# Attention's exponentials turned by a product with a diagonal of one over their sums

## The chip, the cores and the metric

The kernel runs on one core of one Trainium2 chip. The metric is device time of one execution in microseconds (us); the figure for a kernel is the median of its runs. Engines are named as in the profile: PE is TensorE's matmul row, PEld its weight loads, DVE is VectorE, ACT is ScalarE, POOL is GpSimd, SP is SyncE.

## What is computed

Two transformer-like blocks on 256 tokens of width 1024, all in 32-bit floats. The first block holds a forgetting attention with 8 heads of 128 (queries against keys, causal, two blocks of 128 queries), beside it a gated delta rule, and then a feed-forward part. The second holds an attention with 8 heads of 64 over a 4 x 64 grid, beside it a pooling, and again a feed-forward part. What matters here are the two softmaxes and the products that follow them:

```python
# forgetting attention, per head and block of 128 queries
s = jnp.einsum('bhqd,bhkd->bhqk', qi, kh).astype(jnp.float32) * scale
s = s + (ci[..., :, None] - c[..., None, :])
p = jax.nn.softmax(jnp.where(causal, s, -jnp.inf), axis=-1)
return jnp.einsum('bhqk,bhkd->bhqd', p.astype(vh.dtype), vh)
# neighbourhood attention, per head
p = jax.nn.softmax(s.reshape(B, H, GRID_W, wr * WIN_COLS), axis=-1)
return jnp.einsum('bqhwk,bwqkhd->bqhd', p, vg)
```

## The kernel before

The program is written out by hand for the five engines, one function for each: `tensor_program`, `scalar_program`, `vector_program`, `pool_program` and `sync_program`. All big products with weights go through one list of weight panels, cut into half panels (`HALVES`), and every engine walks the same steps n = 1, 2, ... `STEPS`, one for each half panel. In step n, PE does `gemm(n)`; ACT and DVE split the half panel of step n + 3 into a high part (`panel_hi`, line 946) and a rest (`panel_lo`, line 1385), and the high and low parts are multiplied in three products each. There are four buffers for half panels, so the splits stay up to three steps ahead of PE. Everything else is hung on fixed steps: after its big product, each engine does the small pieces that its tables name for this n. The order of every engine's queue is thus written out, and waits are on semaphores of the engine that makes or frees a buffer.

The forgetting attention ("fox") starts head hh at step 39 + 3 hh (`FOX_AT`). In that step PE makes the scores. One step later DVE adds the bias and takes the row maxima (`fox_bias`, line 1586, into `fox_p`, a ring of 3). Two steps later ACT takes exponentials in place and their row sums (`fox_exp`, line 1085). Three steps later DVE inverts the sums and multiplies them in (`fox_normalise`, lines 1590 to 1598). Four steps later PE turns the three 128 x 128 blocks of `fox_p` by transposes against the identity (`fox_turn`, line 769), and ACT copies the result from the PSUM bank to `fox_pT`. Five steps later PE multiplies with the values (`fox_values`); `fox_values(7)` comes in step 64, right behind the turning of head 7. The PSUM banks of scores, turned blocks and results of this attention are a ring of two. In the same steps DVE inverts small matrices for the delta rule (`blocks_X`, `blocks_T`, lines 1546 and 1549), and PE does that rule's products.

The neighbourhood attention ("na") is a staircase over v = 0 to 12 (`NA_AT`): scores and bias of head v, exponentials of head v - 1 (`na_exp`), normalising of head v - 2 (`na_normalise`, lines 1682 to 1689), turning of head v - 3 (`na_turn`, line 816, four blocks of 128 x 128), values from v - 5 on (`na_values`). In two steps more than one v is done with no big product between them (6 and 7, and 11 and 12). Its PSUM banks are a ring of four ("side"), its `na_p` a ring of four.

Of the kernel before, what the change touches and what calls it, by code (L numbers as in the profile page):

```python
# [19 lines left out]
ALU = mybir.AluOpType  # L20
# [3 lines left out]
P = 128  # L24
T = 256
TT = T // P
# [127 lines left out]
FOX_AT = {39 + 3 * hh: hh for hh in range(HEADS)}  # L154
# [30 lines left out]
def build(nc, a, out, scratch_a, scratch_x, scratch_c):  # L185
    ctx = ExitStack()
    with ctx:
        def sem(name):
            return ctx.enter_context(nc.semaphore(name))
# [3 lines left out]
        def at(name, shape, unit, dt=F32, skip=0):  # L193
            return nc.alloc_sbuf_tensor_at(name, shape, dt, offset=BASE + int(unit * UNIT) + skip)[:]
# [8 lines left out]
        fox_p = [at(f"fox_p{i}", [P, 3 * P], 10, skip=1536 * i) for i in range(3)]  # L203
# [53 lines left out]
        na_p = [at(f"na_p{i}", [P, TT, T], 13, skip=2048 * i) for i in range(4)]  # L257
        na_pT = [at(f"na_pT{i}", [P, TT, T], 14, skip=2048 * i) for i in range(4)]

        small_at = [BASE + 25 * UNIT]  # L260

        def small(name, shape, dt=F32, bytes_=4):
            n = bytes_
            for s in shape[1:]:
                n *= s
            t = nc.alloc_sbuf_tensor_at(name, shape, dt, offset=small_at[0])[:]
            small_at[0] += -(-n // 32) * 32
            return t
# [3 lines left out]
        cst = small("constants", [P, N_CONSTS])  # L272
        prm = small("params", [P, N_PARAMS])
        st = small("stats", [P, 176])

        blkA = at("blocks_A", [P, BLOCK, BLOCK], 0, skip=5120)
        blkX = at("blocks_X", [P, BLOCK, BLOCK], 0, skip=6144)
# [12 lines left out]
        def C(name):  # L290
            lo, hi = CONSTS[name]
            return cst[:, lo:hi]
# [5 lines left out]
        ident, upper, ones = C("ident"), C("upper"), C("ones")[:, 0:1].broadcast_to([P, P])  # L298
# [20 lines left out]
        nst = st[:, 48:48 + 32].rearrange("p (h c) -> p h c", c=4)  # L319
# [10 lines left out]
        def fox_stats(hh):  # L330
            return st[:, 128 + 4 * hh:130 + 4 * hh], st[:, 130 + 4 * hh:132 + 4 * hh]

        FOX_PARTS = [slice(0, P), slice(P, 3 * P)]
# [34 lines left out]
        def conv_rows(c):  # L368
# [36 lines left out]
        s_osq, s_oss, s_o_ms, s_o_rs = sem("o_squares"), sem("o_square_sums"), sem("o_means"), sem("o_rsqrt")  # L405
        s_ogz, s_on = sem("o_times_gz"), sem("o_normalised")
        s_yg_hi = sem("yg_hi")
        s_fox_exp, s_fox_rec, s_fox_norm = sem("fox_exp"), sem("fox_reciprocal"), sem("fox_normalised")
        s_yf_hi = sem("yf_hi")
        s_gate_f, s_gate_g, s_mixed, s_y_hi, s_y = (sem(n) for n in ("gate_f_affine", "gate_g_affine", "mixed", "y_hi",  # L410
                                                                      "y_lo"))
# [6 lines left out]
        s_h2_row, s_h2 = sem("h2_row_scaled"), sem("h2_gained")  # L418
        s_n_sq, s_n_ss, s_n_ms, s_n_rs, s_n_tok = (sem(f"qk2_{n}") for n in ("squares", "sums", "means", "rsqrt",
                                                                            "normalised"))  # L420
        s_na_exp, s_na_rec, s_na_norm = (sem(f"na_{n}") for n in ("exp", "reciprocal", "normalised"))
        s_na_hi, s_pool_hi = sem("na_hi"), sem("pooled_hi")
        s_g_tanh, s_g_stt, s_g_mul, s_g_hi, s_g_lo = (sem(f"ffn2_{n}") for n in ("tanh", "silu", "product", "hi", "lo"))
        s_out = sem("output_written")
# [7 lines left out]
        def bank_for(ring, key):  # L432
            while True:
                n = rings[ring][ring_at[ring] % len(rings[ring])]
                ring_at[ring] += 1
                if n not in held:
                    break
            place[key] = (n, uses[n])
            uses[n] += 1
            return banks[n]  # L440
# [4 lines left out]
        def room(key):  # L445
            n, use = place[key]
            return [(s_emptied[n], use)] if use else []

        def filled(key):
            return s_filled[place[key][0]], fill[key]  # L450
# [8 lines left out]
        def will_fill(key):  # L459
            n = place[key][0]  # L460
            times[n] += 1
            fill[key] = times[n]
            return s_filled[n]
# [8 lines left out]
        def side(key):  # L472
            return bank_for("side", key)
# [4 lines left out]
        def pairs(bank):  # L478
            return bank.rearrange("p (c t) -> p c t", c=2)
# [43 lines left out]
        def tensor_program(e):  # L523
# [238 lines left out]
            def fox_turn(hh):  # L762
                key = ("fox_t", hh)
                bank = bank_for("fox", key)
                for s, v in room(key):
                    e.wait_ge(s, v)
                e.wait_ge(s_fox_norm, hh + 1)
                for u in range(3):
                    i_ = e.transpose(bank[:, u * P:(u + 1) * P], fox_p[hh % 3][:, u * P:(u + 1) * P], ident)
                i_.then_inc(will_fill(key), 1)  # L770

            def fox_values(hh):
# [35 lines left out]
            def na_turn(hh):  # L808
                key = ("na_t", hh)
                c3 = pairs(side(key))  # L810
                for s, v in room(key):
                    e.wait_ge(s, v)
                e.wait_ge(s_na_norm, hh + 1)
                for k in range(2):
                    for m in range(TT):
                        i_ = e.transpose(c3[:, k, m * P:(m + 1) * P], na_p[hh % 4][:, m, k * P:(k + 1) * P], ident)  # L816
                i_.then_inc(will_fill(key), 1)

            def na_values(hh):
# [50 lines left out]
            for n in range(1, STEPS + 1):  # L870
# [37 lines left out]
                if n - 4 in FOX_AT:  # L908
                    fox_turn(FOX_AT[n - 4])
# [467 lines left out]
        def vector_program(e):  # L1377
# [209 lines left out]
                                                nm[:, m:m + 1])  # L1587
                i_.then_inc(empties(("fox_s", hh)), 1)

            def fox_normalise(hh):  # L1590
                _, sums = fox_stats(hh)
                pb = fox_p[hh % 3]
                e.wait_ge(s_fox_exp, hh + 1)
                e.reciprocal(sums, sums).then_inc(s_fox_rec, 1)
                e.wait_ge(s_fox_rec, hh + 1)
                for m, s in enumerate(FOX_PARTS):
                    i_ = e.tensor_scalar(pb[:, s], pb[:, s], sums[:, m:m + 1], None, ALU.mult)
                i_.then_inc(s_fox_norm, 1)

            def fox_lo(hh):  # L1600
                e.wait_ge(s_yf_hi, hh + 1)
# [68 lines left out]
            def na_bias(hh):  # L1670
                pb, nm = na_p[hh % 4], nst[:, hh, 0:2]
                b3 = pairs(bank_of(("na_s", hh)))
                if hh >= 4:
                    e.wait_ge(*filled(("na_t", hh - 4)))
                e.wait_ge(s_rpb_masked, hh + 1)
                e.wait_ge(*filled(("na_s", hh)))
                for m in range(TT):
                    i_ = e.tensor_tensor_reduce(pb[:, m, :], b3[:, m, :], bias2[:, hh, m, :], -1.0, -3 * NEG, ALU.add,
                                                ALU.min, nm[:, m:m + 1])
                i_.then_inc(empties(("na_s", hh)), 1)  # L1680

            def na_normalise(hh):
                pb, sums = na_p[hh % 4], nst[:, hh, 2:4]
                e.wait_ge(s_na_exp, hh + 1)
                e.reciprocal(sums, sums).then_inc(s_na_rec, 1)
                e.wait_ge(s_na_rec, hh + 1)
                for m in range(TT):
                    i_ = e.tensor_scalar(pb[:, m, :], pb[:, m, :], sums[:, m:m + 1], None, ALU.mult)
                i_.then_inc(s_na_norm, 1)

            def na_lo(hh):
                e.wait_ge(s_na_hi, hh // 2 + 1)
                e.tensor_tensor(mixl[:, hh // 2, :], bank_of(("na_y", hh // 2))[:, 0:T],
                                mixh[:, hh // 2, :].bitcast(F32), ALU.subtract).then_inc(empties(("na_y", hh // 2)), 1)

            def pool_mean(g):
                e.wait_ge(*filled(("pool_m", g)))
                e.tensor_copy(poolT[:, g, :], bank_of(("pool_m", g))[:, 0:T]).then_inc(empties(("pool_m", g)), 1)

            def pool_lo(g):  # L1700
                e.wait_ge(s_pool_hi, g + 1)
                e.scalar_tensor_tensor(mixl[:, 4 + g, :], bank_of(("pool_y", g))[:, 0:T], PR("pool_scale")[:, g:g + 1],
                                       mixh[:, 4 + g, :].bitcast(F32), ALU.mult, ALU.subtract) \
                    .then_inc(empties(("pool_y", g)), 1)
# [41 lines left out]
            for n in range(1, STEPS + 1):  # L1746
# [118 lines left out]
                if n - 5 in FOX_AT and FOX_AT[n - 5] < 7:  # L1865
                    fox_lo(FOX_AT[n - 5])
                if n - 3 in FOX_AT:
                    fox_normalise(FOX_AT[n - 3])
                if n - 1 in FOX_AT:
                    fox_bias(FOX_AT[n - 1])  # L1870
                for j in range(4):
# [74 lines left out]
                for v in NA_AT.get(n, ()):  # L1946
                    for hh in VALUES_AT.get(v, ()):
                        if hh % 2:
                            na_lo(hh)
                    if 0 <= v - 2 < HEADS:  # L1950
                        na_normalise(v - 2)
                    if 0 <= v < HEADS:
                        na_bias(v)
                    if v - 1 in POOL_AT:
                        pool_lo(POOL_AT[v - 1])
                    if v in POOL_AT:
                        pool_mean(POOL_AT[v])
# [203 lines left out]
        tensor_program(nc.tensor)  # L2161
        scalar_program(nc.scalar)
        vector_program(nc.vector)
        pool_program(nc.gpsimd)
        sync_program(nc.sync)
# [73 lines left out]
```

## Time and profile before

| | us |
|---|---|
| median of 3 runs | 850.86 (849.62 to 851.27) |
| the profiled execution | 851.71 |
| its span | 850.4 |
| PE busy in the span | 828.2 (97%) |
| DVE busy | 584.4 (69%) |
| ACT busy | 442.9 (52%) |
| POOL busy | 87.8 (10%) |

The profile is one execution. The span is what the profiler saw between the first and the last instruction; the profiled execution took 1.3 us more than it. Times in the views below are us from the start of the span. A row of a timeline gives the start, the time taken, engine, line, operation, output and inputs, the count of merged instructions, and in brackets how long the engine had sat idle before and what released it. A 32-bit product that is not a transpose stands in the trace as two matmuls with two weight loads, a transpose as one of each.

### The profile page before, as it was taken

What the parts mean: (1) busy time and instruction counts of PE and PEld (TensorE: products, weight loads), DVE (VectorE), ACT (ScalarE), POOL (GpSimd) and SP (SyncE); (2) the same over time, 40 slices, a digit from 0 to 9 for tenths busy, and PEclk for the clock granted to TensorE, in tenths of its full rate; (3) what the DMA queues carried; (4) which work ended last, traced back from release to release, by engine and by line L of the source; (5) the groups of instructions that cost most, each with busy time, mean ns of one, the idle gap of its engine ahead of it and who ended that gap; (6) DMA issues with size and microseconds to landing.
All of it is one profiled execution on the core that took longest, in us unless ns stands there. A gap on an engine that the chain in (4) does not pass through costs nothing.

```text
span 850.4 us, 14646 instructions
## 1 busy us (share of the span) xinstructions
PE 828.2 (97%) x5992; PEld 773.1 (91%) x5992; DVE 584.4 (69%) x930; ACT 442.9 (52%) x686; POOL 87.8 (10%) x70
## 2 busy tenths in 40 slices
PE   7899999999999999999999999998999999999998
PEld 5899999999998999899999988876767999999887
DVE  5788878784442756669999996586645766666543
ACT  5666577763344344456565563374554444444431
POOL 0001000101010401100211110133000101111000
PEclk9999999999999999999999999999999999999999
DMA  8754563646331465574777665645323755665542
GB/s 245 229 152 150 176 219 115 175 129 176 109 106 50 137 205 159 195 245 151 223 222 251 210 222 175 214 134 172 99 75 87 236 181 169 197 186 168 194 171 75
DMA packets 130707, 144.19 MB, mean 170 GB/s; under 512 B 11456, under 2 KB 111952, under 8 KB 130384
## 3 DMA queue, kind: packets, MB, share of 16 engines
q1 hardware_dynamic: 130640, 143.25, 53.4%
q8 instruction: 48, 0.79, 0.4%
q14 instruction: 19, 0.16, 0.1%
HBM read 141.78 MB, written 1.46 MB: 168 GB/s over the span
## 4 chain that ended last, share of the span: by engine, by line
PE 87%; DVE 5%; issue 3%; ACT 2%; POOL 1%; DMA 1%; SPq 0%; ACTq 0%; POOLq 0%; DVEq 0%
PE bank L525 84%; DVE panel_lo L1385 2%; DMA panel_raw<-in_w_in 1%; POOL stats L1973 1%; ACT panel_hi L946 1%; POOL o_tok L2023 1%; DVE xlo L1406 1%; DMA h<-in_x 1%; PE bank L816 1%; PE bank L566 0%; PE bank L588 0%; PE bank L641 0%; DVE blocks_T L1546 0%; DVE decayT L1448 0%; DVE h L1619 0%
## 5 line engine op out<-in xcount | busy, mean ns | idle before, releaser
L1385 DVE TENSOR_TENSOR panel_lo<-panel_raw,panel_hi 128x1024 fp32r<-128x1024 f32 x252 | 327.2, 1301 | 178.1 <-ACT panel_hi L946 177.2
L946 ACT ACTIVATE panel_hi<-panel_raw 128x1024 fp32r<-128x1024 f32 x252 | 266.7, 1060 | 220.6 <-PE bank L525 214.0
L525 PE MATMUL bank<-xhi,panel_hi 128*128 128x256 f32 x1152 | 329.5, 286 | 4.3 <-ACT conv_acc L946 2.4
L525 PE MATMUL bank<-xhi,panel_lo 128*128 128x256 f32 x1152 | 325.9, 283 | 0.0
L525 PE MATMUL bank<-xlo,panel_hi 128*128 128x256 f32 x1152 | 325.9, 283 | 0.0
L525 PEld LDWEIGHTS bank<-xhi,panel_hi 128*128 128x128 f32 x1152 | 220.9, 192 | 5.2 <-ACT conv_acc L946 2.6
L525 PEld LDWEIGHTS bank<-xlo,panel_hi 128*128 128x128 f32 x1152 | 221.0, 192 | 0.2
L525 PEld LDWEIGHTS bank<-xhi,panel_lo 128*128 128x128 f32 x1152 | 220.9, 192 | 0.0
L525 PE MATMUL bank<-panel_hi,act_hi 128*128 128x512 f32 x176 | 68.6, 390 | 0.0
L525 PE MATMUL bank<-panel_hi,act_lo 128*128 128x512 f32 x176 | 68.5, 389 | 0.0
L525 PE MATMUL bank<-panel_lo,act_hi 128*128 128x512 f32 x176 | 68.5, 389 | 0.0
L525 PE MATMUL bank<-panel_hi,xhi 128*128 128x256 f32 (+1 forms) x192 | 63.8, 333 | 0.8 <-DVE xlo L1406 0.8
L525 PE MATMUL bank<-panel_hi,xlo 128*128 128x256 f32 (+1 forms) x192 | 61.8, 322 | 0.0
L525 PE MATMUL bank<-panel_lo,xhi 128*128 128x256 f32 (+1 forms) x192 | 61.7, 321 | 0.0
L525 PEld LDWEIGHTS bank<-panel_hi,xhi 128*128 128x128 f32 x192 | 36.8, 192 | 4.7 <-issue 2.2
L525 PEld LDWEIGHTS bank<-panel_lo,xhi 128*128 128x128 f32 x192 | 36.9, 192 | 2.8
L525 PEld LDWEIGHTS bank<-panel_hi,act_hi 128*128 128x128 f32 x176 | 33.0, 188 | 6.8
L525 PEld LDWEIGHTS bank<-panel_lo,act_hi 128*128 128x128 f32 x176 | 33.0, 188 | 6.8
L525 PEld LDWEIGHTS bank<-panel_hi,act_lo 128*128 128x128 f32 x176 | 33.0, 188 | 6.8
L525 PEld LDWEIGHTS bank<-panel_hi,xlo 128*128 128x128 f32 x192 | 37.0, 192 | 2.4
L1973 POOL TENSOR_TENSOR stats<-stats 128x2 f32<-128x2 f32 (+1 forms) x9 | 18.1, 2006 | 190.3 <-DVE stats L1399 106.6
L1419 DVE SCALAR_TENSOR_TENSOR conv_acc<-conv_tmp,params,conv_acc 128x255 f32<-128x255 f32 (+2 forms) x72 | 30.4, 479 | 0.0
(280 smaller groups left out, 1059.1 us busy)
## 6 DMA issues: line engine op xcount, KB each, us to landing
panel_raw<-in_w_in SPq DMA_DIRECT2D x38, 1024.0 KB, 5.3
panel_raw<-in_w_up SPq DMA_DIRECT2D x30, 1024.0 KB, 5.3
panel_raw<-in_w_down SPq DMA_DIRECT2D x20, 1024.0 KB, 5.1
panel_raw<-in_w_gate SPq DMA_DIRECT2D x10, 1024.0 KB, 5.3
panel_raw<-in_w_out SPq DMA_DIRECT2D x8, 1024.0 KB, 5.1
panel_raw<-in_w_in SPq DMA_DIRECT2D x12, 512.0 KB, 4.4
panel_raw<-in_w_branch_fox SPq DMA_DIRECT2D x4, 1024.0 KB, 5.1
panel_raw<-in_w_branch_gdn SPq DMA_DIRECT2D x4, 1024.0 KB, 5.2
```

What stands on the lines that cost most here:

```text
L525: return e.matmul(o, l, r, start=start, stop=stop, skip_group_check=True)
L816: i_ = e.transpose(c3[:, k, m * P:(m + 1) * P], na_p[hh % 4][:, m, k * P:(k + 1) * P], ident)
L946: return e.activation(o, i_, ACT.Copy, scale=scale)
L1385: e.tensor_tensor(lo, panel_view(raw[i % 3], PLAN[i][2], k0, kt), hi.bitcast(F32), ALU.subtract).then_inc(s_lo, 1)
L1406: i_ = e.scalar_tensor_tensor(xlo[:, f, :], b3[:, k, :], gain[:, f:f + 1], xhi[:, f, :].bitcast(F32), ALU.mult, ALU.subtract)
L1419: e.scalar_tensor_tensor(acc[:, f, back:], tmp[:, f, 0:T - back], gconv(p, f, back), acc[:, f, back:], ALU.mult, ALU.add).then_inc(s_taps, 1)
L1973: return e.tensor_tensor(cols, cols, minus_half.broadcast_to([P, n]), ALU.pow)
L2023: e.tensor_tensor(tile_of(o_tok, m), tile_of(o_tok, m), gz[:, m].rearrange("p (h d) -> p h d", h=HEADS), ALU.mult).then_inc(s_ogz, 1)
```

## The change

`fox_p` and `na_p` are no longer normalised before they are turned. DVE inverts the sums as before and then scales the identity's rows with them, into a 128 x 128 diagonal for each of the two row blocks of a head (`fox_diag`, one buffer; `na_diag`, two). PE no longer transposes the exponentials against the identity but multiplies them with the diagonal, as ordinary products of 32-bit floats: with the exponentials as stationary operand E, E^T times the diagonal is the turned and normalised block. Steps, order and all other code stay. New are two waits of DVE ahead of the reciprocal: the diagonal of a fox head waits until the head before has been turned, that of an na head until the head two before has been turned.

```diff
+        na_diag = [at(f"na_diag{i}", [P, TT, P], 15, skip=1024 * i) for i in range(2)]
...
+        fox_diag = small("fox_diag", [P, TT, P])
...
-                e.wait_ge(s_fox_norm, hh + 1)
+                e.wait_ge(s_fox_diag, hh + 1)
                 for u in range(3):
-                    i_ = e.transpose(bank[:, u * P:(u + 1) * P], fox_p[hh % 3][:, u * P:(u + 1) * P], ident)
+                    i_ = mm(bank[:, u * P:(u + 1) * P], fox_p[hh % 3][:, u * P:(u + 1) * P], fox_diag[:, (u + 1) // 2, :])
...
-                e.wait_ge(s_na_norm, hh + 1)
+                e.wait_ge(s_na_diag, hh + 1)
                 for k in range(2):
                     for m in range(TT):
-                        i_ = e.transpose(c3[:, k, m * P:(m + 1) * P], na_p[hh % 4][:, m, k * P:(k + 1) * P], ident)
+                        i_ = mm(c3[:, k, m * P:(m + 1) * P], na_p[hh % 4][:, m, k * P:(k + 1) * P],
+                                na_diag[hh % 2][:, m, :])
...
-            def fox_normalise(hh):
-                _, sums = fox_stats(hh)
-                pb = fox_p[hh % 3]
+            def fox_diagonal(hh):
+                if hh:
+                    e.wait_ge(*filled(("fox_t", hh - 1)))
+                sums = fox_stats(hh)[1]
                 e.wait_ge(s_fox_exp, hh + 1)
                 e.reciprocal(sums, sums).then_inc(s_fox_rec, 1)
                 e.wait_ge(s_fox_rec, hh + 1)
-                for m, s in enumerate(FOX_PARTS):
-                    i_ = e.tensor_scalar(pb[:, s], pb[:, s], sums[:, m:m + 1], None, ALU.mult)
-                i_.then_inc(s_fox_norm, 1)
+                for m in range(TT):
+                    i_ = e.tensor_scalar(fox_diag[:, m, :], ident, sums[:, m:m + 1], None, ALU.mult)
+                i_.then_inc(s_fox_diag, 1)
...
-            def na_normalise(hh):
-                pb, sums = na_p[hh % 4], nst[:, hh, 2:4]
+            def na_diagonal(hh):
+                if hh >= 2:
+                    e.wait_ge(*filled(("na_t", hh - 2)))
+                sums = nst[:, hh, 2:4]
                 e.wait_ge(s_na_exp, hh + 1)
                 e.reciprocal(sums, sums).then_inc(s_na_rec, 1)
                 e.wait_ge(s_na_rec, hh + 1)
                 for m in range(TT):
-                    i_ = e.tensor_scalar(pb[:, m, :], pb[:, m, :], sums[:, m:m + 1], None, ALU.mult)
-                i_.then_inc(s_na_norm, 1)
+                    i_ = e.tensor_scalar(na_diag[hh % 2][:, m, :], ident, sums[:, m:m + 1], None, ALU.mult)
+                i_.then_inc(s_na_diag, 1)
```

## Rows read from the trace of the kernel before

**Rows 1.** The page: busy time by engine; the chain that ended last.

```profile
PE 828.2 (97%) x5992; PEld 773.1 (91%) x5992; DVE 584.4 (69%) x930; ACT 442.9 (52%) x686; POOL 87.8 (10%) x70
...
PE 87%; DVE 5%; issue 3%; ACT 2%; POOL 1%; DMA 1%; SPq 0%; ACTq 0%; POOLq 0%; DVEq 0%
```

**Rows 2.** Groups of PE by shape: busy us, mean ns, idle before.

```profile
L816 PE MATMUL bank<-constants,na_p 128*128 128x128 f32 x32 | 5.1, 281 | 0.9 <-DVE mix_lo L1693 0.9
...
L769 PE MATMUL bank<-constants,fox_p 128*128 128x128 f32 x24 | 4.0, 276 | 0.0
```

**Rows 3.** Timeline of PE: 16 plain products, and what follows.

```profile
139.40 3.74 PE L525 MATMUL bank<-kT 128*128 128x128 f32 x32
142.89 0.36 PE L525 MATMUL bank<-xhi,panel_hi 128*128 128x256 f32 x1
```

**Rows 4.** Timeline of PE: 16 transposes, and what follows.

```profile
295.80 1.91 PE L641 MATMUL bank<-constants,o_tok 128*128 128x128 f32 x16
297.46 0.36 PE L525 MATMUL bank<-yf_hi,panel_hi 128*128 128x256 f32 x1
```

**Rows 5.** Timeline of PE: head 0 of fox is turned.

```profile
162.23 0.49 PE L769 MATMUL bank<-constants,fox_p 128*128 128x128 f32 x3
```

**Rows 6.** A group of DVE by shape: busy us, mean ns, idle before.

```profile
L1597 DVE TENSOR_SCALAR fox_p<-fox_p,stats 128x128 f32<-128x128 f32 x8 | 2.5, 311 | 0.3
```

**Rows 7.** Timeline of DVE at head 1 of fox.

```profile
172.00 0.55 DVE L1597 TENSOR_SCALAR fox_p<-fox_p,stats 128x128 f32<-128x128 f32 x2
172.47 1.22 DVE L1385 TENSOR_TENSOR panel_lo<-panel_raw,panel_hi 128x1024 fp32r<-128x1024 f32 x1
```

**Rows 8.** Timeline of PE: turning and values of head 1.

```profile
172.69 0.52 PE L769 MATMUL bank<-constants,fox_p 128*128 128x128 f32 x3
...
176.75 0.94 PE L525 MATMUL bank<-fox_pT,vf 128*128 128x128 f32 x6 [0.67 <-DVE stats L1586]
```

**Rows 9.** The chain ahead of that wait: start, us, what.

```profile
166.29 0.03 ACT yf_hi L946
```

**Rows 10.** Timeline of all engines: head 4 of fox is turned.

```profile
213.32 0.49 PE L769 MATMUL bank<-constants,fox_p 128*128 128x128 f32 x3
213.52 0.60 ACT L946 ACTIVATE X<-bank 128x512 f32<-128x512 f32 x1 [0.28 <-PE bank L641]
...
214.26 0.52 PE L525 MATMUL bank<-X,BT 128*128 128x64 f32 x3 [0.45 <-ACT X L946]
```

**Rows 11.** Timeline of all engines: head 7 of fox is turned.

```profile
272.74 0.49 PE L769 MATMUL bank<-constants,fox_p 128*128 128x128 f32 x3
273.41 0.48 ACT L946 ACTIVATE fox_pT<-bank 128x384 f32<-128x384 f32 x1
...
273.99 0.91 PE L525 MATMUL bank<-fox_pT,vf 128*128 128x128 f32 x6 [0.76 <-issue]
```

**Rows 12.** The chain in the na stretch: start, us, what.

```profile
621.88 0.70 ACT v L946
...
623.89 0.59 PE bank L816 x4
...
634.12 0.44 DVE mix_lo L1693
...
634.60 0.66 PE bank L816 x4
```

**Rows 13.** Timeline of DVE: sums of head 5 of na are inverted.

```profile
627.44 0.15 DVE L1685 RECIPROCAL stats<-stats 128x2 f32<-128x2 f32 x1
```

**Rows 14.** Timeline of PE around its wait of 3.37 us.

```profile
585.24 1.07 PE L792 MATMUL bank<-constants,qk 128*128 128x128 f32 x8 [3.37 <-DVE qk L1667]
...
587.38 0.63 PE L525 MATMUL bank<-panel_hi,xhi 128*128 128x512 f32 x1
...
590.24 0.39 PE L525 MATMUL bank<-panel_lo,xhi 128*128 128x512 f32 x1
```

**Rows 15.** Window: us; busy by engine; granted clock, DMA share, GB/s.

```profile
587.00:588.00 1.00, 1.00 (x4) 0.81 (x3) 0.00 (x0) 1.00 (x3) 0.00 (x0) 0.50 0.00 0
```

More of the change, by code:

```diff
@@ L407, in build @@
         s_yg_hi = sem("yg_hi")
-        s_fox_exp, s_fox_rec, s_fox_norm = sem("fox_exp"), sem("fox_reciprocal"), sem("fox_normalised")
+        s_fox_exp, s_fox_rec, s_fox_diag = sem("fox_exp"), sem("fox_reciprocal"), sem("fox_diagonal")
         s_yf_hi = sem("yf_hi")
@@ L420, in build @@
                                                                             "normalised"))
-        s_na_exp, s_na_rec, s_na_norm = (sem(f"na_{n}") for n in ("exp", "reciprocal", "normalised"))
+        s_na_exp, s_na_rec, s_na_diag = (sem(f"na_{n}") for n in ("exp", "reciprocal", "diagonal"))
         s_na_hi, s_pool_hi = sem("na_hi"), sem("pooled_hi")
@@ L1867, in vector_program @@
                 if n - 3 in FOX_AT:
-                    fox_normalise(FOX_AT[n - 3])
+                    fox_diagonal(FOX_AT[n - 3])
                 if n - 1 in FOX_AT:
@@ L1950, in vector_program @@
                     if 0 <= v - 2 < HEADS:
-                        na_normalise(v - 2)
+                        na_diagonal(v - 2)
                     if 0 <= v < HEADS:
```

## The prediction, made before the changed kernel ran

> **What bounds the kernel now.** I read the page first: PE is busy 97% of the span and carries 87% of the chain that ended last; the next engine, DVE, has 5% of that chain [rows 1]. PE's timeline shows why: it has few gaps in which it waited for anybody, and between them one matmul follows on the other. So what the change adds to PE's queue lengthens the kernel, unless it lies directly ahead of a gap whose end is set by another engine; and what it takes off DVE shortens the kernel only where DVE ends such a gap. The next view is therefore PE's timeline at each turning, to see whether a gap follows, and the last is the chain through these gaps, to see whether the work that ends a gap was itself started by PE behind a turning.
>
> **PE: 56 transposes become 56 products.** 24 blocks of fox_p and 32 of na_p are turned, each by one matmul [rows 2]. The duration in such a row (276 and 281 ns) is latency and not the price, since matmuls overlap; the price is the distance between starts. A plain 32-bit product of the same size stands twice in the trace: 16 of them are 32 matmuls, from 139.40 to 142.89 [rows 3], 3.49 us, or 0.218 us each. 16 transposes take 295.80 to 297.46 [rows 4], 1.66 us, or 0.104 each. The difference is 0.114 us for a block, 3 x 0.114 = 0.34 us for a fox head, 4 x 0.114 = 0.46 for an na head, and 56 x 0.114 = 6.4 us for all of it. Nothing else is on PE at that time that could hide it: a weight load is tied to each of these matmuls, and the rows compared hold their loads already. Bounds for a block: 0.104 from below (exactly a second pass at a transpose's distance), and 0.13 from above (if the whole 3.74 us of rows 3 were the price of its 16 products); I take 0.114, since form, size and type are those of rows 3 and starts are what PE's queue is paced by.
>
> **Where it hides.** Three fox heads have a gap right behind them.
> Head 1 is turned at 172.69, and PE then waits 0.67 us until 176.75, for DVE to free the bank that the scores of head 2 held [rows 8]. That DVE work descends from the ACT copy at 166.29, which PE had released behind the turning of head 0 [rows 9]: the delay of head 0 reaches it, that of head 1 does not. Head 1's 0.34 us fits into 0.67 and is hidden.
> Head 4 is turned at 213.32, and PE waits 0.45 us for the ACT copy of X that began at 213.52 and hangs on transposes ahead of the turning [rows 10]. ACT does that copy before it looks at head 4, so 0.34 us is hidden here too, with 0.1 to spare.
> Head 7 is turned at 272.74, its last transpose ends at 273.23, but ACT is busy and starts the copy only at 273.41; PE waits 0.76 us for it [rows 11]. 0.34 us later the copy starts at about 273.60: 0.19 is paid and 0.15 hidden.
> The other five fox heads are followed by big products without a gap and pay in full. In the na stretch there are two gaps. That at 621.88 waits for ACT to bring v out of its bank behind the last product of v2, later by whatever PE is later; the head turned at 623.89 comes after it. That before 634.60 ends with mix_lo on DVE, behind values that PE had just made; again the turning follows it [rows 12]. Nothing hides in either, and all eight heads pay 0.46.
>
> **DVE.** Instead of 128 x 128 and 128 x 256 (fox), or twice 128 x 256 (na), it now writes twice 128 x 128. On DVE's timeline the fox pair takes its place from 172.00 to 172.47, 0.47 us [rows 7]. A 128 x 128 one is a row of 311 ns [rows 6] and overlaps its neighbour; I estimate the new pair at 0.40, between 0.33 (nothing but a bit over one row) and 0.47. The 0.07 (0 to 0.14) saved counts once, in the DVE-bound stretch before 176.75. In the na stretch the saving is perhaps 0.13 a head, but there DVE waits for others ahead of the gap that it ends, so it is worth nothing. ACT, POOL, SP and their queues do the same work in the same places.
>
> **The two new waits** stand on DVE ahead of the reciprocal, and the split that follows would be queued behind them, and PE behind the split. They are met long before: the diagonal of fox head 1 is due at about 171.8, head 0 was turned at 162.23 [rows 5]. The narrowest place is na head 5, due at 627.44 [rows 13], which needs head 3 turned: the transposes of 623.89 end at 624.48 [rows 12], with the change at 624.9. 2.5 us remain. Cost 0; if that cover were gone, DVE would stand still, and PE after it only when three splits had been used up. Turning in its turn waits for the diagonal and no longer for the normalised block, which comes no later than before.
>
> **The sum** against the profiled execution: fox 8 x 0.34 = 2.7, less 0.34 + 0.34 + 0.15 and 0.07, makes 1.8; na 8 x 0.456 = 3.65. Together +5.5 us, 851.71 to 857.2. The median of the runs before is 0.85 us under the profiled execution, so the median after is expected at 850.86 + 5.5 = 856.4.
>
> **The clock.** After a wait of 3.37 us at 585.24 the matmuls of the next product take 0.63 instead of 0.39 us, with the granted clock at 0.50, the lower of the two levels [rows 14, 15]; eight of them make 8 x 0.24, at most 1.9 us. The wait lies before the na turnings and behind the fox ones, and the change shifts it by 1.8 us without changing its length. Whether the clock falls there in every execution a single trace can't say; the runs before differ by 1.65 us, about this much. I take it as unchanged, and as 1.9 us of width to either side, less likely in the median of several runs.
>
> **Rivals.**
> *The product costs no second pass.* If a product with a 128 x 128 diagonal went through PE at a transpose's 0.104 us, nothing of 6.4 us would be left, and only DVE's saving would count: 0 to -0.1 us, 850.8, not slower. It decides at each of the 56 blocks: one matmul in the trace for a product, not two. For it speaks only that a transpose is by form also a product with a constant. Against it: every plain 32-bit product here stands doubled, 32 for 16 [rows 3].
> *The gaps swallow more.* If the gaps at 621.88 and 634.60 (0.87 and 0.93 us) did not move with PE, and heads behind them were caught up, some 1.8 us less would be paid: +3.7, 854.6. Against it: both gaps end with work that PE itself released [rows 12].
> *A transpose is much cheaper than a product.* With three more passes for a block in place of one, 56 x 3 x 0.104 = 17.5 us, less the gaps behind heads 1, 4 and 7 (1.3 us at most and 0.1 for DVE), +16, 866.9. Against it rows 3 and 4: 0.218 to 0.104 is a factor of 2.1. The Trainium skill, "TensorE: Matmul & The Clock Gate", section Terms, says of the transpose mode that it is four times faster for FP32; by that rule a block would go from 0.104 to 0.42 us and the kernel to 866.9. The trace doesn't agree: a factor of 2.1.
> *A new wait.* If a diagonal's buffer came free late, DVE's split and then PE would stand; for the narrowest place this needs 2.5 us more delay than I see, and would then cost parts of a us on top: 857 to 859.
>
> **How the numbers follow.** Full price of 6.4 us within a few tenths, less what hides: 88%, 856.4. No second pass 3%; gaps swallow more 4%; three more passes 2%; a new wait 3%. From the forecast's own bounds: everything hidden that could be, 854.6, and a clock that does not fall, 854.5; below that 0.5 for the scatter of a median: 854.0. Above: nothing hidden is 850.86 + 6.4 = 857.3, and the upper bound for a block (56 x 0.13 = 7.3) or a worse clock up to 1 more: 858.3. About 0.2% (1.7 us) is what a measurement of this kernel can tell from no change. The forecast, the swallowing gaps, the passes and the new wait are all slower by more than that, with some width lost to the unknown: slower 0.94, within 0.2% 0.05, faster 0.01.
>
> **What the profile after would show.** Right: the turnings stand as 48 and 64 matmuls with about 0.11 us from start to start, PE's busy time is up by some 6 us, the gap ahead of the values of head 1 is shorter by about 0.4 us and that behind head 4 nearly gone, na turnings take 0.9 us in place of 0.44; DVE's rows of the diagonal are 128 x 128 and no reciprocal waits for a turning. Wrong: 24 and 32 matmuls for the turnings, or four each; gaps of PE that have grown; DVE idle before a reciprocal; or a clock below full in the fox or na stretch, where it is full now.

## The result, and the profile after

The changed kernel took 857.24 us (median of 6 runs, 856.71 to 858.05), the kernel before in 6 runs 851.28 (849.62 to 854.28): 5.96 us slower, ratio 1.0073 with a 95% interval of 1.0059 to 1.0086. Forecast were 856.4 us and +5.5. The profiled execution took 857.02 us, forecast 857.2.

The page of the changed kernel, busy time by engine and the chain that ended last:

```profile
span 855.7 us, 14771 instructions
...
PE 834.9 (98%) x6048; PEld 780.7 (91%) x6048; DVE 583.1 (68%) x930; ACT 443.2 (52%) x686; POOL 87.9 (10%) x70
...
PE 87%; DVE 5%; issue 3%; ACT 2%; POOL 1%; DMA 1%; SPq 0%; ACTq 0%; POOLq 0%; DVEq 0%
```

PE has 56 matmuls more (6048 for 5992) and is busy 6.7 us longer; DVE is busy 1.3 us less; the shares of the chain are what they were [rows 1]. The turnings and the diagonals, from the groups by shape of the changed kernel (busy us, mean ns, idle before):

```profile
L528 PE MATMUL bank<-na_diag,na_p 128*128 128x128 f32 x64 | 8.9, 283 | 0.9 <-DVE mix_lo L1701 0.9
...
L528 PE MATMUL bank<-fox_diag,fox_p 128*128 128x128 f32 x48 | 6.9, 280 | 0.0
...
L1603 DVE TENSOR_SCALAR fox_diag<-constants,stats 128x128 f32<-128x128 f32 x16 | 4.1, 298 | 0.3
...
L1696 DVE TENSOR_SCALAR na_diag<-constants,stats 128x128 f32<-128x128 f32 x16 | 3.9, 284 | 0.3
```

48 and 64 matmuls stand where 24 and 32 stood [rows 2]: a second pass for each block, no more. To see where the time went, I cut both traces at the same places of PE's program. The marks, from PE's timeline of the kernel before (two more are in rows 11 and 14):

```profile
158.70 0.82 PE L525 MATMUL bank<-kfT,qfT 128*128 128x128 f32 x4
...
593.28 1.13 PE L525 MATMUL bank<-k2T,q2T 64*128 64x256 f32 x4
...
646.61 1.09 PE L525 MATMUL bank<-na_pT,v 128*64 128x256 f32 x8
```

and from PE's timeline of the changed kernel:

```profile
158.22 0.82 PE L528 MATMUL bank<-kfT,qfT 128*128 128x128 f32 x4
...
176.55 0.94 PE L528 MATMUL bank<-fox_pT,vf 128*128 128x128 f32 x6 [0.27 <-DVE stats L1590]
...
275.56 0.91 PE L528 MATMUL bank<-fox_pT,vf 128*128 128x128 f32 x6 [0.69 <-issue]
...
586.80 1.94 PE L795 MATMUL bank<-constants,qk 128*128 128x128 f32 x8 [3.37 <-DVE qk L1673]
...
594.73 1.13 PE L528 MATMUL bank<-k2T,q2T 64*128 64x256 f32 x4
...
651.93 1.09 PE L528 MATMUL bank<-na_pT,v 128*64 128x256 f32 x8
```

| stretch | before | after | difference |
|---|---|---|---|
| start to scores ahead of fox head 0 turning | 158.70 | 158.22 | -0.48 |
| fox: from there to the values of head 7 | 115.29 | 117.34 | +2.05 |
| to the first turning of qk | 311.25 | 311.24 | 0 |
| clock: from there to the first na scores | 8.04 | 7.93 | -0.11 |
| na: from there to the last values | 53.33 | 57.20 | +3.87 |
| to the end of the span | 203.8 | 203.8 | 0 |

All of the loss lies in the two stretches with turnings, +5.92 us. The span shows 5.3, since this execution was 0.48 us earlier at the first mark, ahead of any changed instruction, and 0.11 us shorter in the clock stretch. The start and the clock stretch differ between executions of the same code. The other stretches agree to 0.05 us between the two executions of the changed kernel (e9 below is the second), so the experiments are read by the fox and na stretches beside their medians. One caution: the fox stretch of e4, whose fox code is that of the kernel before, is 0.29 us longer, and that of e8 0.63. Nearly all of each lies in a single head, so fox is also read head by head.

The fox heads one by one, as the distance from the values of one head to those of the next (for head 0 from the first mark): 6.72, 11.33, 10.37, 17.32, 19.86, 13.57, 12.57, 23.55 us before, and 7.07, 11.26, 10.73, 17.71, 19.86, 13.97, 12.91, 23.83 after. Each distance belongs to the turning that lies in it. Head 1 and head 4 pay nothing, the gap ahead of 176.55 has shrunk from 0.67 to 0.27 [rows 8], and the row behind head 4 names no idle time any more [rows 10], as this piece of PE's timeline of the changed kernel shows:

```profile
213.86 0.83 PE L528 MATMUL bank<-fox_diag,fox_p 128*128 128x128 f32 x6
214.81 0.41 PE L528 MATMUL bank<-X,BT 128*128 128x64 f32 x2
```

### The profile page after: what moved, and what is told of

It is laid out like the page before. It is cut to its first block, busy times and chain, and to the rows that moved or that the text cites. A ratio compares the mean times of both kernels' runs of the same rounds, so it can differ in the third digit from the quotient of the medians.

```text
span 855.7 us, 14771 instructions
## 1 busy us (share of the span) xinstructions
PE 834.9 (98%) x6048; PEld 780.7 (91%) x6048; DVE 583.1 (68%) x930; ACT 443.2 (52%) x686; POOL 87.9 (10%) x70
## 4 chain that ended last, share of the span: by engine, by line
PE 87%; DVE 5%; issue 3%; ACT 2%; POOL 1%; DMA 1%; SPq 0%; ACTq 0%; POOLq 0%; DVEq 0%
PE bank L528 86%; DVE panel_lo L1389 2%; DMA panel_raw<-in_w_in 1%; ACT panel_hi L950 1%; POOL stats L1981 1%; POOL o_tok L2031 1%; DVE xlo L1410 1%; DMA h<-in_x 1%; PE bank L569 0%; PE bank L591 0%; PE bank L644 0%; PE bank L795 0%; DVE blocks_T L1550 0%; DVE decayT L1452 0%; DVE h L1625 0%
```

## The experiments

The theory: PE's second pass for each block is the whole loss, less what hides in PE's gaps behind fox heads 1, 4 and in part 7. The rivals: the diagonals, their writes or their waits on DVE take or give a part; nothing hides; or a pass costs something else on the path than its distance between starts. Medians and ratios are against runs of the kernel before on the same chip; "fox" and "na" are the differences of the two stretches to the kernel before, and "clock" that of the clock stretch.

| kernel | median (before) | ratio, 95% interval | fox | na | clock |
|---|---|---|---|---|---|
| changed | 857.24 (851.28) | 1.0073, 1.0059 to 1.0086 | +2.05 | +3.87 | -0.11 |
| e1 products alone | 858.66 (851.24) | 1.0082, 1.0068 to 1.0095 | +2.11 | +3.91 | +1.13 |
| e2 diagonals alone | 851.18 (851.24) | 1.0001, 0.9988 to 1.0015 | +0.20 | 0.00 | -1.57 |
| e3 fox only | 853.30 (851.24) | 1.0023, 1.0011 to 1.0034 | +1.94 | +0.06 | +1.30 |
| e4 na only | 855.20 (851.24) | 1.0041, 1.0027 to 1.0055 | +0.29 | +3.90 | +0.03 |
| e9 changed again | 857.21 (851.72) | 1.0066, 1.0049 to 1.0084 | +2.03 | +3.92 | -0.26 |
| e10 products again | 856.55 (851.72) | 1.0055, 1.0039 to 1.0071 | +2.10 | +3.92 | -1.57 |
| e6 products twice | 868.13 (851.72) | 1.0197, 1.0177 to 1.0218 | +6.32 | +11.07 | +0.04 |
| e7 transposes twice | 857.05 (851.72) | 1.0061, 1.0043 to 1.0080 | +1.99 | +3.51 | +0.05 |
| e8 heads 1 and 4 | 850.76 (851.26) | 0.9993, 0.9979 to 1.0007 | +0.63 | +0.01 | +0.03 |
| e5 one buffer | 857.30 (851.26) | 1.0067, 1.0044 to 1.0089 | +2.28 | +3.91 | +1.18 |

### The change taken apart

Products alone, in the kernel before:

```diff
-                    i_ = e.transpose(bank[:, u * P:(u + 1) * P], fox_p[hh % 3][:, u * P:(u + 1) * P], ident)
+                    i_ = mm(bank[:, u * P:(u + 1) * P], fox_p[hh % 3][:, u * P:(u + 1) * P], ident)
...
-                        i_ = e.transpose(c3[:, k, m * P:(m + 1) * P], na_p[hh % 4][:, m, k * P:(k + 1) * P], ident)
+                        i_ = mm(c3[:, k, m * P:(m + 1) * P], na_p[hh % 4][:, m, k * P:(k + 1) * P], ident)
```

> The kernel before, but its 56 turnings are plain products with the identity in place of transposes; DVE normalises as before. My theory (PE's second pass is the whole loss): 56 blocks at 0.11 to 0.12 us more, less what hides behind heads 1, 4 and 7 of fox: +5.6 to +6.0 us against the kernel before, ratio 1.0065 to 1.0071; the turnings stand as 48 and 64 matmuls. Rival (the diagonal, its two waits or its writes on DVE are a part of the loss): this kernel is faster than the changed one by more than 1 us, so +4.9 or less.

Diagonals alone, in the changed kernel:

```diff
-                    i_ = mm(bank[:, u * P:(u + 1) * P], fox_p[hh % 3][:, u * P:(u + 1) * P], fox_diag[:, (u + 1) // 2, :])
+                    i_ = e.transpose(bank[:, u * P:(u + 1) * P], fox_p[hh % 3][:, u * P:(u + 1) * P], ident)
...
-                        i_ = mm(c3[:, k, m * P:(m + 1) * P], na_p[hh % 4][:, m, k * P:(k + 1) * P],
-                                na_diag[hh % 2][:, m, :])
+                        i_ = e.transpose(c3[:, k, m * P:(m + 1) * P], na_p[hh % 4][:, m, k * P:(k + 1) * P], ident)
```

> The changed kernel, but PE turns by transposes against the identity; DVE makes the diagonals with the two new waits, and nobody multiplies with them: the normalisation is left out of the output. My theory: 0 to -0.2 us against the kernel before, with the gap of PE ahead of the values of fox head 1 shorter by 0.07 us. Rival (the new waits or the diagonals cost time): slower than before by more than 1 us, and DVE idle ahead of a reciprocal.

The products alone bring the whole loss in the trace, 2.11 + 3.91 = 6.02 us against 5.92 of the changed kernel. The diagonals alone bring none by their runs (1.0001); their na stretch is 53.33 us, exactly that before, and no reciprocal waited. Their fox stretch is 0.20 longer instead of 0.07 shorter, 0.17 of it ahead of the values of head 1 (11.50 for 11.33). That piece is uneven in itself: e4 has the fox code of the kernel before and 11.62 there, while six traces with products in all fox heads have 11.17 to 11.35 and e5, the seventh, 11.49. In seven of the twelve traces a panel_lo in this piece took 1.32 to 1.54 us in place of 1.22, as here in DVE's timeline of e2 and of e4 (one row each):

```profile
167.57 1.47 DVE L1388 TENSOR_TENSOR panel_lo<-panel_raw,panel_hi 128x1024 fp32r<-128x1024 f32 x1 [0.71 <-ACT panel_hi L949]
```

```profile
167.44 1.52 DVE L1389 TENSOR_TENSOR panel_lo<-panel_raw,panel_hi 128x1024 fp32r<-128x1024 f32 x1 [0.71 <-ACT panel_hi L950]
```

Why that row is longer in some executions I didn't settle, and it doesn't explain the piece alone: e3 has 1.40 us there and the shortest piece. But there are four traces in which it took 1.22 or 1.23 us and PE still waits behind head 1. Of these, the two with the old normalising have 11.33 (before) and 11.33 us (e10), the two with diagonals 11.26 (changed) and 11.27 (e9). That is the 0.07 us, as far as two pairs can tell, and e2 alone doesn't show it.

But the medians of the products alone said something else: 858.66 against 857.24 for the changed kernel, 1.4 us more, as if the diagonal gave that back. It was the rival's number, though the two intervals of the table overlap. The two traces, 1.31 us apart, had the difference in one place, the clock stretch (9.17 us against 7.93), where neither kernel has a changed instruction. So both ran again, side by side.

> The changed kernel itself, once more, beside the next one on the same chip. My theory (the diagonal differs from the identity for PE in nothing, and what DVE saves is 0.07 us): +5.9 against the kernel before, and within 0.5 us of the products with the identity once the clock behind the wait of 3.4 us is the same in both. Rival (normalising on DVE costs more than I see, so the diagonal gives back over 1 us): this kernel is 1 to 1.5 us faster than the next one, with a trace that shows the difference elsewhere than at the clock.

> Products with the identity in place of transposes, DVE as in the kernel before; once more, beside the changed kernel. My theory: +6.0 against the kernel before, as much as the changed kernel within 0.5 us. Rival: 1 to 1.5 us slower than the changed kernel, as the medians of the first comparison had it.

This time the products alone were the faster ones, 856.55 against 857.21, with overlapping intervals, and the stretches with turnings agree once more (6.02 and 5.95). The rival falls: a product with the diagonal cost PE as much as one with the identity, to 0.1 us over all 56. Between the two traced executions of the first comparison the clock stretch made 1.24 of the 1.31 us; that it also made the difference of the medians is likely but not shown, since the other executions have no trace.

### The change in each attention by itself

e3 keeps the new code of the first block and has the kernel before's `na_normalise` and `na_turn`; e4 is the reverse.

```diff
-                if hh >= 2:
-                    e.wait_ge(*filled(("na_t", hh - 2)))
...
-                    i_ = e.tensor_scalar(na_diag[hh % 2][:, m, :], ident, sums[:, m:m + 1], None, ALU.mult)
+                    i_ = e.tensor_scalar(pb[:, m, :], pb[:, m, :], sums[:, m:m + 1], None, ALU.mult)
```

> The change in the forgetting attention alone (24 blocks). My theory, from the shifts between the two traces: +2.0 us (1.8 as predicted, 2.05 as the traces differ), ratio 1.0023, with 0 behind head 4 and -0.07 behind head 1. Rival (nothing hides, each block pays): +2.8.

> The change in the neighbourhood attention alone (32 blocks). My theory: +3.65 as predicted, +3.9 as the traces differ, ratio 1.0043 to 1.0046, about 0.43 to 0.46 for heads turned among big products and 0.50 for those behind the values of another head. Rival (the gaps of 0.87 and 0.93 us take up some of it): +3 or less.

The parts add up: 1.94 us in fox and 3.90 in na, 5.84 together, and 2.1 + 4.0 us by the medians. Fox is nearer to 2.0 than to the 2.8 of a kernel in which nothing hides; in na nothing hides, and the two gaps of 0.87 and 0.93 us stayed as long as they were and moved with PE, which refutes the rival of swallowing gaps. PE's timeline of the changed kernel has them so:

```profile
625.49 1.18 PE L528 MATMUL bank<-na_pT,v 128*64 128x256 f32 x8 [0.87 <-ACT v L950]
...
638.39 1.16 PE L528 MATMUL bank<-na_diag,na_p 128*128 128x128 f32 x8 [0.93 <-DVE mix_lo L1701]
```

### The price of a pass

e6 makes each product of the changed kernel twice into the same place, e7 each transpose of the kernel before:

```diff
-                for u in range(3):
+                for u in (0, 1, 2) * 2:
...
-                for k in range(2):
+                for k in (0, 1) * 2:
```

> The changed kernel with each of the 56 products made twice into the same place. My theory: 0.222 us for each more, less what is left of the gap ahead of the values of fox head 1 (0.27): +12.2 against the changed kernel, +18.1 against the kernel before, ratio 1.0213. Rival (weight loads or banks limit, and the first product carries a cost of its own): 8 or less, or 15 or more, against the changed kernel.

> The kernel before with each of its 56 transposes made twice. My theory: 0.104 to 0.11 us for each more, less about 0.33 behind each of fox heads 1 and 4 and 0.1 behind head 7: +5.1 to +5.4 against the kernel before, ratio 1.0060 to 1.0064, a little under the changed kernel. Rival (a transpose costs less on the path than its distance between starts): +3 or less.

In the na stretch, where nothing hides, 32 more products cost 11.07 - 3.87 = 7.20 us, 0.225 for a block, and 32 more transposes 3.51 us, 0.110. Both medians are as the distances between starts had it for transposes (+5.3, expected 5.1 to 5.4) and a little under it for products (+10.9 against e9, expected +12.2; the trace has 4.27 + 7.20 = 11.5). The miss is in fox: I had let head 1 hide only 0.27 us more and head 4 nothing. Yet with products twice the piece of head 1 still took 11.29 us, and that of head 4 20.18, 0.32 more for 0.67 more of PE's time. So 0.64 of the 0.67 us was hidden at head 1 and 0.35 at head 4, where the matmuls' rows of the changed kernel name 0.27 us and nothing as idle. The rows of the weight loads name more. In the changed kernel they had sat idle 0.15 us ahead of the turning of head 1 and 0.48 ahead of the values behind it, together 0.63, and 0.27 behind head 4 (0.08 less than was hidden there, which stays open):

```profile
172.47 0.74 PEld L528 LDWEIGHTS bank<-fox_diag,fox_p 128*128 128x128 f32 x6 [0.15 <-issue]
...
176.55 0.74 PEld L528 LDWEIGHTS bank<-fox_pT,vf 128*128 128x128 f32 x6 [0.48 <-DVE stats L1590]
...
214.77 3.65 PEld L528 LDWEIGHTS bank<-X,BT 128*128 128x128 f32 x32 [0.27 <-issue]
```

The same load had 0.66 us in the kernel before, for 0.45 of the matmul:

```profile
214.23 0.52 PEld L525 LDWEIGHTS bank<-X,BT 128*128 128x128 f32 x4 [0.66 <-issue]
```

A transposed block in this kernel thus costs 0.110 us and a multiplied one 0.225 to 0.231 (0.110 + 3.87/32): a factor of 2.1. The Trainium skill, "TensorE: Matmul & The Clock Gate", section Terms, has the transpose mode four times faster for FP32. The runs here don't agree: they measure the factor of 2.1.

### Are the gaps behind heads 1 and 4 free?

```diff
+                    if hh in (1, 4):
+                        i_ = mm(bank[:, u * P:(u + 1) * P], fox_p[hh % 3][:, u * P:(u + 1) * P],
+                                fox_diag[:, (u + 1) // 2, :])
+                    else:
+                        i_ = e.transpose(bank[:, u * P:(u + 1) * P], fox_p[hh % 3][:, u * P:(u + 1) * P], ident)
```

> The kernel before with the change for fox heads 1 and 4 alone (6 of 56 blocks), the two with a gap of PE right behind them. My theory: their 0.68 us on PE is hidden, and 0.07 is saved on DVE, so 0 to -0.2 us between PE's step ahead of head 0 and the values of head 7, and no change that runs can show; the gap ahead of the values of head 1 is 0.27 in place of 0.67, the one behind head 4 is gone. Rival (the gaps only look free): +0.7 between the same two places of the trace.

By the runs yes: 0.9993, with an interval that ends at 1.0007, +0.6 us, just under the rival's +0.7. By the number alone the trace sides with the rival, +0.63 us in the fox stretch. Head by head it doesn't: 11.38 for 11.33 with head 1, 19.90 for 19.86 with head 4, and the 0.54 us are all in the piece of head 3 (17.86 for 17.32), which is turned by transposes here. There PE waited for DVE, and DVE for the key bias of head 4. PE's and DVE's timelines of e8 at this place:

```profile
204.52 0.71 PE L528 MATMUL bank<-fox_pT,vf 128*128 128x128 f32 x4 [0.37 <-DVE stats L1593]
```

```profile
203.82 0.29 DVE L1593 CUSTOM_DVE_ANT_0 fox_p<-bank,key_bias 128x128 f32<-128x128 f32 x1 [7.40 <-POOL key_bias L1992]
```

and the chain that ended last in e8 ahead of it (start, us, what):

```profile
195.88 6.88 DMA key_bias<-gate_sums
...
202.83 0.88 POOL key_bias L1992 x2
```

The chain there goes through SP's queue, a DMA of 6.88 us and POOL. In the kernel before, DVE had waited 6.52 us for the same key bias and was done 0.4 us before PE needed it; in the changed kernel PE comes 0.5 us later anyway. This is a limit close behind PE that I had not seen. In the twelve traces DVE gets this key bias 44.7 to 45.9 us behind the first mark; with every product made twice, and PE 1.9 us later at the turning of head 3 than in the kernel before, it is 45.4. So it doesn't move with the turnings, but it scatters by 1.2 us (0.6 between the two traces of the changed kernel), and in e8 it came late (45.6) and last. The six products of heads 1 and 4 cost 0.05 and 0.04 us.

### What a tighter wait would cost

```diff
-                if hh >= 2:
-                    e.wait_ge(*filled(("na_t", hh - 2)))
+                if hh >= 1:
+                    e.wait_ge(*filled(("na_t", hh - 1)))
```

and one na_diag in place of two.

> The changed kernel with one diagonal buffer in place of two for the neighbourhood attention, so that each diagonal waits until the head before has been turned, which PE does in the same step. My theory: DVE now waits ahead of reciprocals, 1 to 3 us in all, but PE has three splits ahead of it and the scores that DVE needs next come behind the same turning: 0 to +0.5 us against the changed kernel. Rival (a wait of this kind on DVE goes to the end): +1 us or more against the changed kernel, with new gaps of PE that DVE ends.

DVE's waits in e5, 603 to 655 us (total, times, longest):

```profile
DVE stats L1693 <- PE bank L528: 6.8, 6, 1.6
```

DVE stood 6.8 us ahead of its reciprocals, more than the 1 to 3 I expected, and the na stretch took 57.24 us against 57.20. DVE's waits for scores in this stretch shrank meanwhile, from 9.3 us in the changed kernel to 4.7. What was queued behind the waits, the bias of the next head, needed scores that PE makes behind the same turning, and the splits stayed ahead. A DVE that waits there as long as this costs nothing; in the changed kernel it doesn't even wait. The longer span of this execution (857.0) is the clock stretch, 9.22 us.

## Why the prediction was right, point by point

- **What bounds the kernel**: right. PE's queue sets the end, and what was added to it came out at the end but for gaps set by others.
- **The price of a block**: right in kind, a little small. 0.114 us were expected; the three na heads that follow big products show 0.43, 0.46 and 0.46 us (0.456 expected), but the five behind the values of another head 0.48 to 0.52. That makes na +3.87 for the 3.65 of the sum. Why products cost some 0.05 us a head more there I didn't settle; the transposes at this place were dearer too (0.59 for 0.44 in the chain).
- **Fox heads in full**: 0.35, 0.36, 0.39, 0.40 and 0.34 us for heads 0, 2, 3, 5 and 6, for 0.34 each: 0.14 too little together. Why heads 3 and 5 pay 0.05 more is open.
- **Heads 1 and 4 hidden**: right; e8 and e6 show it, and there was more room than I counted.
- **Head 7 in part**: 0.28 paid, not 0.19. The copy by ACT began 0.10 us after the last product's modelled end, and I had let it follow after 0.03. This and the line above are the 0.23 between 1.82 and 2.05.
- **DVE's saving**: the pair takes 0.40 us (171.87 to 172.27 on DVE's timeline of the changed kernel) for 0.47, as estimated. Two pairs of traces show it in PE's distance behind head 1 (11.33 to 11.26, 11.33 to 11.27); more can't be said, since that piece varies by 0.4 between traces.

```profile
171.87 0.48 DVE L1603 TENSOR_SCALAR fox_diag<-constants,stats 128x128 f32<-128x128 f32 x2
172.27 1.22 DVE L1389 TENSOR_TENSOR panel_lo<-panel_raw,panel_hi 128x1024 fp32r<-128x1024 f32 x1
```

- **The new waits**: right, cost 0, and e5 shows a far wider margin than the 2.5 us I gave.
- **The clock**: held as "unchanged", which came true for the two traces compared (8.04 and 7.93). That was luck: other traces had 1.57 us less or 1.30 more, inside the 1.9 us given to either side.
- **The rival of three more passes** is refuted by e6 and e7, that of no second pass by the 112 matmuls, that of swallowing gaps by e4, that of a wait by e2 and e5.

The median landed 0.8 above 856.4 and inside the range: 0.4 of it from the terms named, 0.4 since the kernel before also came out at 851.28 in more runs.

## What to carry to other kernels

Where TensorE's queue is the bound, turning a 32-bit block by a product instead of a transpose costs a second pass, here 0.115 us for each 128 x 128 block, with the identity as with a diagonal; folding a scale into it buys time only if the engine freed of the scaling is the one that is waited for. Price such an edit by the distance between starts in a run of equal instructions, subtract the heads with a gap whose end another engine sets, and look whether that engine's work was itself released behind the turning. A median difference of a microsecond between two kernels on this kernel's scale should be located in the traces before it is explained: here, in the executions traced, it sat in a stretch neither had changed.

## What the runs showed of the hardware

After the same wait of 3.4 us for qk, TensorE's granted clock took one of three courses in executions of nearly the same program: it stayed at full, 2.4 GHz (clock stretch 6.47 us, in e2 and e10), fell to half, 1.2 GHz, for about 3.4 us (7.8 to 8.1 us: before, changed, e4, e6 to e9), or for about 6.8 us (9.2 to 9.3: e1, e3, e5). Windows of e3 show the long one (us; busy by engine; granted clock, DMA share, GB/s):

```profile
587.00:588.00 1.00, 0.67 (x4) 0.70 (x5) 1.00 (x2) 0.00 (x0) 0.00 (x0) 0.50 0.63 242
...
592.00:593.00 1.00, 1.00 (x4) 0.75 (x3) 0.81 (x1) 1.00 (x2) 0.00 (x0) 0.50 0.00 0
```

and a window of e2, in the same big product, full clock:

```profile
587.00:588.00 1.00, 1.00 (x6) 0.83 (x5) 0.00 (x0) 1.00 (x3) 0.00 (x0) 1.00 0.07 16
```

The first and the third are 2.7 to 2.9 us apart, half of what the change cost. Which one comes does not follow from the kernel: the same code as e1 took the third course in e1 and the first in e10. I had expected one fall and at most 1.9 us from it.

There is a second such place near the start. Behind a wait of PE of 1.9 us that ends at 13.2 to 13.8 us, the clock fell to half for about 3.4 us in e4, e6 and e10, while it stayed at full in the other nine traces. One window of e4, and the same of the kernel before:

```profile
16.00:17.00 1.00, 1.00 (x7) 1.00 (x6) 1.00 (x4) 0.59 (x1) 0.00 (x0) 0.50 1.03 332
```

```profile
16.00:17.00 1.00, 1.00 (x10) 1.00 (x10) 1.00 (x4) 0.52 (x1) 0.00 (x0) 1.00 1.09 299
```

It can't be seen in the times: those three traces reach the first mark at 157.3 to 157.7 us, the other nine at 157.7 to 158.9. So a lower mean clock of an execution doesn't say by itself that it lost time.
